# mLSTM, gated and attention stages: another order of work, latent norms partly on GpSimd, stores waited for later

## The reference, cut to what matters

```python
y_a = g * jax.nn.sigmoid(g @ w_glu) * jax.nn.silu(z_a)          # gated stage
def _rms(x, g):                                                # latent norms of c_q (384) and c_kv (256)
    y = xf * lax.rsqrt(jnp.mean(xf * xf, axis=-1, keepdims=True) + EPS)
...
a = jax.nn.silu(conv + conv_b)                                 # mLSTM branch, 4 heads of 256
q = jnp.einsum('blhd,hde->bhle', a, w_q)
k = jnp.einsum('blhd,hde->bhle', a, w_k) * (MLSTM_DH ** -0.5)
h_f = _mlstm_dir(q, k, v, i_f, log_sigmoid(f_f)); h_b = _flip(_mlstm_dir(_flip(q), ...))
y_c = sigmoid(o_c) * _head_rms(h_f + h_b, c_norm) * silu(z_c)
...
return jnp.concatenate([y_c, y_d], axis=-1) @ w_out
```

## Time and profile before

| | us |
|---|---|
| median of three runs (range) | 3396.75 (3393.96 to 3398.62) |
| the profiled execution: its own time | 3399.88 |
| its span | 3398.3 |
| mean granted TensorE clock | 0.984 |
| TensorE busy, share of the span | 3274.6, 96% |
| VectorE, ScalarE, GpSimd busy | 1674.6, 1429.7, 653.3 |

### The profile page before, as it was taken

How to read it: one execution, slowest core, us unless ns; L and a number is a source line. 1 busy time by engine, 2 the same in 40 slices (tenths; PEclk the granted TensorE clock), 3 DMA queues, 4 the chain that set the end, 5 groups by cost and what they waited for, 6 DMA issues and landing times. The chain is left out here.

```text
span 3398.3 us, 44207 instructions
## 1 busy us (share of the span) xinstructions
PE 3274.6 (96%) x16490; PEld 2721.3 (80%) x16490; DVE 1674.6 (49%) x3113; ACT 1429.7 (42%) x2567; POOL 653.3 (19%) x452
## 2 busy tenths in 40 slices
PE   7999999989799999999999999999999997998999
PEld 6788888877688888788888888888888886886887
DVE  4899999835755565521323223232322514665311
ACT  5233232233466676510235645455554225554200
POOL 4212121111201111033231111111112112331231
PEclk9999999999899999999999999999999999999999
DMA  4333333276521211453333232322322453444521
GB/s 132 89 83 100 85 100 91 77 217 208 176 57 39 58 45 38 118 158 106 112 98 115 86 119 75 126 72 83 114 82 86 152 178 100 138 141 139 173 92 62
DMA packets 431620, 367.07 MB, mean 108 GB/s; under 512 B 76984, under 2 KB 367288, under 8 KB 431408
## 3 DMA queue, kind: packets, MB, share of 16 engines
q1 hardware_dynamic: 346400, 270.64, 27.7%
q10 hardware_dynamic: 85008, 93.61, 7.9%
HBM read 237.29 MB, written 126.86 MB: 107 GB/s over the span
## 5 line engine op out<-in xcount | busy, mean ns | idle before, releaser
L2765 ACT ACTIVATE eow_w1raw<-of_ring 128x512 f32<-128x512 f32 x218 | 126.8, 596 | 397.5 <-PE of_ring L3166 395.4
L873 PE MATMUL ef_ring<-ef_hhi,ef_whi 128*128 128x512 f32 x720 | 289.1, 402 | 1.8 <-issue 1.0
L875 PE MATMUL ef_ring<-ef_hhi,ef_wlo 128*128 128x512 f32 x720 | 281.5, 391 | 0.0
L874 PE MATMUL ef_ring<-ef_hlo,ef_whi 128*128 128x512 f32 x720 | 281.5, 391 | 0.0
L399 POOL TENSOR_TENSOR ef_wlo<-ef_wraw,ef_whi 128x1024 fp32r<-128x1024 f32 x29 | 85.3, 2942 | 484.7 <-ACT ef_whi L448 484.7
L2992 DVE SCALAR_TENSOR_TENSOR of_state<-of_state,of_small,of_tv 128x256 f32<-128x256 f32 x64 | 56.1, 877 | 242.0 <-ACT of_tv L2827 240.0
L873 PEld LDWEIGHTS ef_ring<-ef_hhi,ef_whi 128*128 128x128 f32 x720 | 135.8, 189 | 41.7 <-issue 14.9
L510 ACT ACTIVATE ef_stage<-ef_ring 128x512 f32<-128x512 f32 x90 | 53.5, 594 | 268.0 <-PE ef_ring L875 267.8
L875 PEld LDWEIGHTS ef_ring<-ef_hhi,ef_wlo 128*128 128x128 f32 x720 | 135.8, 189 | 29.4
L874 PEld LDWEIGHTS ef_ring<-ef_hlo,ef_whi 128*128 128x128 f32 x720 | 135.9, 189 | 26.1
L2682 POOL TENSOR_TENSOR eo_w0lo<-of_wraw,eo_w0hi 128x1024 fp32r<-128x1024 f32 x27 | 66.3, 2457 | 453.8 <-ACT eo_w0hi L2719 453.8
(11 more groups left out here) (658 smaller groups left out, 9363.6 us busy)
## 6 DMA issues: line engine op xcount, KB each, us to landing
of_wraw<-o_w_in SPq DMA_DIRECT2D x53, 512.0 KB, 3.9
ef_wraw<-e_w_in SPq DMA_DIRECT2D x29, 512.0 KB, 4.2
s_tmo<-eow_w1raw ACTq DMA_DIRECT2D x48, 256.0 KB, 2.3
ow_raw<-s_yt SPq DMA_DIRECT2D x18, 512.0 KB, 6.0
ow_raw<-o_w_out SPq DMA_DIRECT2D x16, 512.0 KB, 5.0
s_uc<-ef_stage ACTq DMA_DIRECT2D x24, 256.0 KB, 2.6
ef_ut<-s_uc SPq DMA_DIRECT2D x16, 384.0 KB, 4.1
s_za<-ef_stage ACTq DMA_DIRECT2D x24, 256.0 KB, 2.3
```

The lines of the kernel that those rows point to most:

```text
L873: pe.matmul(out, ah, hhi[:, f, tc], start=(f == 0), stop=False)
L874: pe.matmul(out, ah, hlo[:, f, tc], start=False, stop=False)
L875: mm = pe.matmul(out, al, hhi[:, f, tc], start=False, stop=(f == KT - 1))
L2765: act.activation(stage[i % 4][:, :], ring[i % 3][:, :] if i else start.first, func, scale=GK ** -0.5 if name == "q" else 1.0).then_inc(eva ...
```

## The change

In the gated stage the squares are taken two groups earlier (3, 7, 13). GpSimd adds the slices (`sums`): slice 0 to 1 and 3 to 4 in one instruction, then 0 to 2, in place; TensorE does two matmuls a norm and waits for `sum_done`. ScalarE waits at the end for half of the `yt` buffers, (0, 1); buffers (2, 3) are waited for in the attention stage by SyncE, GpSimd, ScalarE and VectorE (`stored`), and VectorE's sign memsets move behind its first subtractions. In the mLSTM stage the first head's groups are evacuated in the order FIRST, the wait for identity and gain is split, the first fades move ahead of four weightings, the turns of a head's tiles 0 to 7 move from between the next head's projections to between the prompt's products, and in the last head the conversions of the output weights and the first products with them move later.

```diff
@@ glu
-    NORM = (8, 12, 18)
+    NORM, SQUARE = (8, 12, 18), (3, 7, 13)
+                def sums(i):
+                    pool.wait_ge(sq_done, i + 1)
+                    pool.tensor_tensor(sq[:, 0:4:3, :], sq[:, 0:4:3, :], sq[:, 1:5:3, :], ALU.add).then_inc(pair_done, 1)
+                    pool.wait_ge(pair_done, i + 1)
+                    pool.tensor_tensor(sq[:, 0, :], sq[:, 0, :], sq[:, 2, :], ALU.add).then_inc(sum_done, 1)
+                for t in range(1, NW):
+                    w_low(t)
+                    sums(t - 1)
-                    if g + 3 in NORM:
-                        square(NORM.index(g + 3))
+                    if g in SQUARE:
+                        square(SQUARE.index(g))
-                for k in range(4):
-                    act.wait_ge(y_out[k], 16 * TG // 4)
+                after.stored(act, (0, 1))
-                    for x, ks in enumerate((range(3), range(3, KC))):
-                        for k in ks:
-                            mm = pe.matmul(acc[i % 2][:, cut(x)], ones[:, :], sq[:, k, :], start=(k == ks[0]), stop=(k == ks[-1]))
-                        mm.then_inc(ss_mm, 1)
+                    for x, k in enumerate((0, 3)):
+                        pe.matmul(acc[i % 2][:, cut(x)], ones[:, :], sq[:, k, :], start=True, stop=True).then_inc(ss_mm, 1)
@@ attention: start.stored(engine, (2, 3)) on SyncE, GpSimd, ScalarE and VectorE
@@ mlstm, ring
-            for g in range(NG):
-                ring_items.append(("p", h + 1, g))
-                ring_items += [("t", NH * h + t) for t in range(2 * g - 6, 2 * g - 4) if t >= 0]
-            ring_items += [("t", NH * h + 6), ("t", NH * h + 7)]
+            ring_items += [("p", h + 1, g) for g in range(NG)]
+            ring_items += [("t", NH * h + i) for i in range(8)]
@@ mlstm, ScalarE
+    FIRST = (0, 1, 4, 2, 3, 5)
-                for g in range(2):
+                for g in FIRST[:3]:
                     evac(0, g)
                 exponents(0)
                 for b in range(2):
                     exps(b)
-                for g in range(2, 4):
+                for g in FIRST[3:]:
                     evac(0, g)
                 for b in range(2, 4):
                     exps(b)
-                for g in range(4, NG):
-                    evac(0, g)
-                act.wait_ge(const_in, 32)
...
-                        root(h, 0)
                         for g in range(NG):
                             evac(h + 1, g)
-                            if g in (1, 2):
-                                exps(NH * (h + 1) + 5 + g)
+                            if g == 0:
+                                root(h, 0)
                             if g >= 2:
                                 scaled(NH * h + 2 * g - 4)
                                 scaled(NH * h + 2 * g - 3)
+                        for b in range(6, 8):
+                            exps(NH * (h + 1) + b)
...
-                            if g == NH * MH - 12:
+                            if g == NH * h + 5:
                                 ahead.high(act, 0)
-                            if g == NH * MH - 10:
-                                ahead.high(act, 1)
...
+                            if i == 0:
+                                ahead.high(act, 1)
@@ mlstm, VectorE
                 for h in range(MH):
...
+                    if h == 0:
+                        for g in range(4):
+                            faded(0, g)
                     for j in range(4):
                         if h:
                             gated(NH * h - 4 + j)
                         weighted(h, NC + j)
-                    if h == 0:
-                        for g in range(4):
-                            faded(0, g)
...
-                        if NH * h + b == NH * MH - 12:
+                        if h + 1 == MH and b == 6:
                             ahead.low(dve, 0)
...
                         for g in range(NG):
                             low(h + 1, g)
                             if g < 4:
                                 faded(h + 1, g)
-                            if g >= 3:
-                                gated(NH * h + 2 * g - 6)
-                                gated(NH * h + 2 * g - 5)
+                            if g == 0:
+                                roots(h, 0)
                         for i in range(4):
                             outputs(NH * h + 8 + i)
-                            if i < 2:
-                                gated(NH * h + 6 + i)
+                            gated(NH * h + 2 * i)
+                            gated(NH * h + 2 * i + 1)
@@ mlstm, TensorE
-                pe.wait_ge(const_in, 32)
...
                         for g in range(NG):
                             project(h + 1, g)
-                            if g >= 3:
-                                turn(NH * h + 2 * g - 6)
-                                turn(NH * h + 2 * g - 5)
-                        for i in range(4):
-                            products(NH * h + 8 + i)
-                            if i < 2:
-                                turn(NH * h + 6 + i)
-                    else:
                         for i in range(4):
                             products(NH * h + 8 + i)
                             turn(NH * h + 2 * i)
                             turn(NH * h + 2 * i + 1)
+                    else:
+                        products(NH * h + 8)
+                        for i in range(3):
+                            products(NH * h + 9 + i)
+                            turn(NH * h + 2 * i)
+                            turn(NH * h + 2 * i + 1)
+                        turn(NH * h + 6)
+                        turn(NH * h + 7)
```

More of the change, by code:

```diff
@@ L168, in __init__, with stored @@
             outer.sem(x) for x in ("first_in", "second_in", "pos_in", "head_in"))
+        self.y_out = [outer.sem(f"y_out{k}") for k in range(4)]
+    def stored(self, eng, ks):
+        for k in ks:
+            eng.wait_ge(self.y_out[k], 16 * 6 * D // W256 // 4)
 def even_front(nc, d, after):
@@ L1016, in glu @@
         gs_done, y_done = s.sem("gs_done"), s.sem("y_done")
-        y_out = [s.sem(f"y_out{k}") for k in range(4)]
+        y_out = after.y_out
         w = start.w
@@ L1092, in _, with w_low @@
             def _(pool):
-                pool.memset(ones[:, :], 1.0).then_inc(one_done, 1)
-                for t in range(1, NW):
+                def w_low(t):
                     u = t % 2
@@ L1434, in _ @@
                 rope_weights(1)
+                start.stored(sp, (2, 3))
                 sp.dma_start(ident[:, :], d["ident"][:, :]).then_inc(const_in, 16)
@@ L1511, in _ @@
                 head_low(0)
+                start.stored(pool, (2, 3))
                 rope_low(0)
@@ L1601, in _ @@
                 latent_high(1)
+                start.stored(act, (2, 3))
                 for x in opening[0:2]:
@@ L1711, in gated @@
                     tt(y[m % 3][:, :], o[:, 0:256], zb[m % 3][:, :], ALU.mult).then_inc(y_done, 1)
+                first_low(0, slice(3, KC))
+                first_low(1, slice(0, 3))
+                latent_low(1)
+                start.stored(dve, (2, 3))
                 dve.memset(sign, 1.0).then_inc(sign_set, 1)
@@ L3754, in _ @@
                     else:
+                        act.wait_ge(ident_in, 16)
                         act.activation(small[:, 500:501], ident[:, 0:1], ACT.Sqrt)
@@ L3869, in gated @@
                                                  gates(g, 0)[:, x, :], ALU.mult, ALU.mult).then_inc(yt_done, 1)
-                for g in range(NG):
+                for g in FIRST:
                     low(0, g)
-                dve.wait_ge(const_in, 32)
                 for h in range(MH):
@@ L3896, in _ @@
                         outputs(NH * h + b)
-                        if NH * h + b == NH * MH - 12:
+                        if h + 1 == MH and b == 6:
                             ahead.low(dve, 0)
-                        if NH * h + b == NH * MH - 10:
-                            ahead.low(dve, 1)
                     means(h, 0)
-                    roots(h, 0)
                     if h + 1 < MH:
@@ L3922, in _ @@
                             last_mean(i)
+                            if i == 0:
+                                ahead.low(dve, 1)
+                        gated(NH * h + 6)
+                        gated(NH * h + 7)
+                        last_scale(2)
+                        last_mean(3)
                         gated(NH * h + 8)
@@ L3985, in turn_keys @@
                     if slot["x", h, j] == 3:
-                        pe.wait_ge(el_done, G0)
+                        pe.wait_ge(el_done, evacuated(0, G0 - 1))
+                    if h == 0 and j == TURNED[0]:
+                        pe.wait_ge(ident_in, 16)
                     pe.wait_ge(a_in[j // 2], 16 * (h + 1))
@@ L4096, in _ @@
                             turn(NH * h + 8 + u)
-                        for u in range(2):
```

(6 more changed lines are left out.)

37 lines of the change are left out of this document (21 added, 16 removed).

## The result

The changed kernel takes 3350.89 us (median of four runs, 3349.68 to 3351.77) beside 3395.64 us (3393.96 to 3398.62) for the kernel before: a ratio of 0.9864, interval 0.9852 to 0.9875, some 45 us less. The profiled execution took 3350.53 us (span 3348.9) at a granted clock of 0.990.

The account below looks back on a forecast made before the run. TensorE, busy 96% of the span, was taken as the bound. Terms 14.5 + 13.2 + 14.3 + 10.9 = 52.9 us off the 3396.75 us median gave 3344; 3336 to 3350 had 0.66, 3334 to 3362 held 8 in 10.

Parts of the forecast that it names:

- Matmuls of the norms: Gated stage: ten sum matmuls a norm become two, so 24 of 0.43 us go, 10.3 us.
- The early squares': Gated stage, first norm: TensorE's 3.9 us wait for squares and 2.7 us of low clock go.
- New waits: Gated stage: TensorE waits 0.8 us for the first sum, 1.0 for a sigmoid, 0.7 for the second sum; 2.5 together.
- The gated stage's end: Three queues: latents' store lands 1 to 2 us behind TensorE; of 14.4 + 1.6 us, 14.5 taken (11 to 16.5).
- The stores' part: Gated stage's end: no longer waiting there for the last stores to land gives 1.6 us, no more.
- The sums block VectorE: Rival, gated stage: GpSimd's adds hold up VectorE's gating products; the stage gives 6 us, total 3352; chance 0.12.
- Turns hand the stall on: Rival, changes of head: waits become waits for late gates at first scores; 17.0 becomes 5, total 3353; chance 0.15.
- The change doesn't remove what it names: Rival, mLSTM start: identity or v as late as the gain, so the 7.3 us wait stays; total 3354; chance 0.05.
- The clock stays low: Rival, mLSTM stage: scattered waits of 0.5 to 3.0 us keep the clock low, making it slower, 3414; chance 0.02.
- Start of the mLSTM stage: First head: waits of 7.3 and 4.9 us and low clock go, 16.7, less new waits: 13.2 us (10 to 14).
- Changes of head: mLSTM stage, three changes: 4.0 us waits and low clock go, 17.0, less 0.9 each: 14.3 us (7.4 to 17).
- Last head: mLSTM stage: 13.9 us of waits and low clock go, one turn 3 us late: net 10.9 us (8 to 13).

Follow-up runs that it names:

- e6_early: Kernel before with only the norms' squares two groups earlier (3, 7, 13), sums still on TensorE: 3390.96 beside 3398.15 us, 0.9980.
- e2_stores: Kernel before with only the later waits for the last two yt buffers: 3397.03 beside 3399.46 us, 0.9995.
- e5_last: Kernel before with only the mLSTM stage's last head changed (conversions, last turns, roots, first output products): 3387.11 beside 3398.15 us, 0.9965.
- e1_gated: Kernel before with only the norms' edits (early squares, sums on GpSimd), all four y_out still waited for: 3391.78 beside 3399.46 us, 0.9976.
- e11_swap: Changed kernel with SyncE issuing the mLSTM stage's gate loads ahead of the stores: 3350.29 us beside 3398.88 us for the kernel before, 0.9853.
- e9_split: Changed kernel, attention's loads split: positions, head weights, first latents after group 17, second latents behind group 21's operands: 3347.31 us beside 3398.88 us before, 0.9847.
- e12_best: Changed kernel with positions and head weights loaded early, latents behind group 21's operands, third square at 14, gate loads before stores: 3345.56 us, 0.9842 to the kernel before.
- e10_tsum: Changed kernel with attention's loads one group earlier and the norms' sums back on TensorE: 3348.30 us beside 3398.88 us for the kernel before, 0.9851.
- e8_loads: Changed kernel with SyncE's loads for attention one group earlier: 3346.99 us beside 3398.15 us for the kernel before, 0.9851.
- e3_start: Kernel before with only the mLSTM stage's start changed (evacuation order, split waits, earlier first fades): 3386.47 beside 3399.46 us, 0.9965.

## Why the prediction was right, and where it was not

**The time.** 3344 was forecast, 3350.9 measured, inside 3334 to 3362 and on the right side. But it lies just outside the narrower 3336 to 3350, and nearer to 3352 and 3353, the times of two rivals; the total alone doesn't tell them from my account, only the marks and the runs do. The sum said 52.9 us, the marks say 45.0. Most of the difference, 6.8 us, is the gated stage's.

**Matmuls of the norms: mis-sized.** 24 x 0.43 = 10.3 us should have gone. The earlier trace rows shows ten logged matmuls for five products in the code; I kept one for one for the two that remain, but they are four:

```profile
757.67 1.98 PE L1224 MATMUL gl_acc<-gl_sq,gl_ones 128*128 128x512 f32 x4 [0.79 <-POOL gl_sq L1112]
781.69 1.98 PE L1224 MATMUL gl_acc<-gl_sq,gl_ones 128*128 128x512 f32 x4 [0.19 <-POOL gl_sq L1112]
```

18 went, worth 3 x 4.45 - 1.98 - 1.98 - 1.88 = 7.5 us. The early squares' 3.9 + 2.7 = 6.6 were right (6.7 in e6_early). New waits were 1.0 for the sums (0.8 at the first, as forecast) and 0.8 for low weights, not 2.5. So 7.5 + 6.6 - 1.8 = 12.3, and 12.4 measured, not 14.4. That the two agree to 0.1 us is luck: the wait for the first squares, 3.9 us in the trace that I read, is 4.3 to 5.7 in e2_stores to e5_last, where nothing ahead of it was changed.

**The gated stage's end: the step that failed.** I had the third norm's end nearly right (843 to 845.5; it was 844.6, in an execution in which the stage begins 2.6 us earlier than before, and 845.7 and 846.0 in e1_gated and e11_swap), took 9.7 us from there to the store's landing, and capped the loss at 1 to 2 us. The landing came 15.1 us behind the norm: 6.4 us until the store was issued, 8.7 until it landed. That left out what stands ahead of the store on SyncE: the operands of group 23, behind attention's loads. The row was there (the store at 858.57, 9.7 us to landing, while the norm's products had ended at 857.0); I read its landing as the price of such a store, where it goes with what else the DMA engines carry: of the three latents' stores before, the two others took half of that, and the third took 4.8 us in e9_split and 5.9 in e12_best, where attention's loads come earlier.

```profile
DMA to landing us min/median/max: 4.8/4.9/9.7
```

A TensorE that is 12 us early moves what feeds this queue by less. The second norm isn't earlier at all: its reciprocal starts at 810.77 us, at 810.07 before. The third's starts at 834.65, at 847.04 before, 9.8 us earlier if each is counted from the stage's first matmul, and attention's loads are issued 7.6 us earlier by the same count:

```profile
810.77 6.57 DVE L1196 RECIPROCAL gl_acc<-gl_acc 128x1024 f32<-128x1024 f32 x1 [2.64 <-ACT gl_acc L1145]
...
834.65 6.57 DVE L1196 RECIPROCAL gl_acc<-gl_acc 128x1024 f32<-128x1024 f32 x1 [0.20 <-ACT gl_acc L1145]
```

So the term gave 7.7 instead of 14.5. The text named this case as what would make it wrong (SyncE's latents' store several us behind TensorE), but gave it no chance and no price. The stores' part, read behind the last matmul, was 1.3 us alone (8.7 to 7.4) and 0.9 on top of e1_gated (14.3 to 13.4); 1.6 was forecast.

**The rivals.** *The sums block VectorE* happens once, at the second norm, as the earlier trace rows let one expect. The Trainium skill (SBUF — State Buffer, "Who interferes with whom") says that a VectorE instruction with two SBUF inputs contends with a GpSimd instruction that reads SBUF. VectorE's two products of group 9 take 2.44 and 1.66 us instead of 0.69 each, each ending just behind an add:

```profile
777.54 2.40 POOL L1110 TENSOR_TENSOR gl_sq<-gl_sq 128x1024 f32<-128x1024 f32 x1 [3.43 <-ACT gl_sq L1141]
780.02 1.61 POOL L1112 TENSOR_TENSOR gl_sq<-gl_sq 128x512 f32<-128x512 f32 x1
...
778.05 2.44 DVE L1207 TENSOR_TENSOR gl_gt<-gl_gt,gl_sg 128x512 f32<-128x512 f32 x1 [2.06 <-ACT gl_sg L1151]
780.53 1.66 DVE L1209 TENSOR_TENSOR gl_gt<-gl_gt,gl_za 128x512 f32<-128x512 f32 x1
```

That is 2.7 us on VectorE's chain; the rule and the trace agree. It is not what kept TensorE's gain from the end: e6_early, without it, starts attention at the same time as e1_gated, and e10_tsum, without it, later than e8_loads. Whether the sums without the collision would end earlier wasn't tried. *Turns hand the stall on*: in small, below. *The change doesn't remove what it names*: no, the 7.3 us went (e3_start). *The clock stays low*: it does behind one of the new waits. The earlier trace rows left gaps of 1.6 to 4.0 us open; behind the 1.7 us gap at 2802.79 the clock is 1.00, behind the 2.1 us gap at 3074.70 it is 0.55 for 3.8 us, 1.7 us that my "3 us late" for that turn didn't count. It needn't be: in e9_split, e10_tsum and e11_swap the clock stays at 1.00 behind the same gap. Nowhere else in the stage is a new wait that long, so the chain of low stretches that the rival needed doesn't arise.

**Start of the mLSTM stage.** 13.2 forecast, 13.7 measured, and 13.7 alone between the same marks (e3_start). The new waits are where I put them: 0.4 and 1.1 before the scores and keys (0.5 and 0.8 forecast), 1.2 at the key updates (1.7), none at the products.

**Changes of head.** 14.3 forecast, 12.7 measured. The new waits are 2.3, 1.8 and 1.4 us, not 0.9 each. At least 1.3 us of them are the late gates that I had followed through eight rounds of SyncE, since e11_swap takes as much away; the rest is open. (In the sum, 3 x 3.5 x 0.47 is 4.9 and not 1.65, which is one change's share; the 17.0 is right.) Against that stand 1.6 us of old waits in the third change that I hadn't counted as gone.

**Last head.** 10.9 forecast, 11.3 measured: the turn is 2.1 us late and costs 1.7 more by the clock, 3 forecast. Without the low clock, as in three of the other kernels, this part is 42.9 us and the gain would be 12.9: that it came out near the forecast is in part luck.

## What to carry to other kernels

When an engine's time in a stage shrinks, ask which queue ends the stage, and follow that queue's issues in order: a store behind someone else's load waits for the load's place in the DMA engines, however early its data is. Loads for the next stage belong into a stretch in which the DMA engines are idle, and with the share at 1.0 moving them by a group gave 3.3 us, less than the 5 to 6 that I expected from the order alone. To judge parts of a few us, measure between marks in the stage itself, since whole executions differ by as much; look in other kernels how much the same part varies untouched, and put the first mark as close before the edit's effect as you can.

## What the runs showed of the hardware that I had not expected

- An instruction that issues a DMA is not always short. A 256 KB load of `za` takes SyncE 0.51 us to issue (837.11 in the changed kernel), and the next one 5.18 us (845.84), with some 4 MB of loads ahead of it.
- The same gap brings the clock down in one execution and not in another. The turn in the last head comes behind a gap of 2.1 us in seven kernels. In the 3.8 us behind it the granted clock is 0.55 in the changed kernel and 0.69 to 0.72 in e5_last, e8_loads and e12_best, but 1.00 in e9_split, e10_tsum and e11_swap, where the last head is 1.6 us shorter (42.9 instead of 44.5). The row of e11_swap:

```profile
3075.70:3079.50 3.80, 3.80 (x21) 3.00 (x21) 3.37 (x15) 2.35 (x8) 0.00 (x0) 1.00 0.66 192
```

- How long TensorE stays slow behind a gap didn't go with the gap's length. At attention's start the first matmuls take 0.63 us and later ones 0.39: from the first of them to the first that takes 0.40 or less it is 3.0 us behind a gap of 13.0 us (863.74 in the changed kernel), 5.6 behind 13.9 (e1_gated), 3.0 behind 8.0 (e9_split) and 6.0 behind 6.6 (e12_best). Behind the same 8.3 us it is 3.5 us in the kernel before and 6.0 in e3_start, whose code is the same up to there.
- Behind code that no edit touched, the gated stage's first matmul starts anywhere from 715.19 to 719.13 us in the fourteen profiled executions.
